# Where the down projections stand among the up projections of a feed-forward stage (fp32 split in two parts, four layers)

## The reference, cut to what matters

```python
# layers 0 and 1, D_FF = 2816
ffn = (jax.nn.silu(x @ w_ffn_gate[l]) * (x @ w_ffn_up[l])) @ w_ffn_down[l]
x = layer_norm(ALPHA * x + ffn, ln2_g[l], ln2_b[l])

# layers 2 and 3, D_FF_2 = 2816
u = h @ w_up                                   # both halves, 5632 columns
up = jnp.pad(u, ((0, 0), (CONV_WIDTH - 1, 0), (0, 0)))
c = conv_b
for j in range(CONV_WIDTH):
    c = c + conv_w[j] * up[:, j:j + S]
val, gate = jnp.split(c, 2, axis=-1)
x = x + (jax.nn.silu(gate) * val) @ w_down
```

## Time and profile before

| | us |
|---|---|
| median of 3 launches | 1415.01 |
| lowest, highest | 1412.89, 1415.77 |
| the profiled execution's own time | 1413.5 |
| span of its one core, first to last instruction | 1411.7 |

### The profile page before, as it was taken

The page is one execution under the profiler, slowest core; times in us unless marked ns, Lnnn a source line. Parts: engine busy times, 40 slices in busy tenths (PEclk is TensorE's granted clock), DMA queues, the critical chain, the costliest instruction groups (busy, mean ns, idle before and its releaser), DMA issues.

```text
span 1411.7 us, 24782 instructions
## 1 busy us (share of the span) xinstructions
PE 1362.0 (96%) x10120; PEld 1251.1 (89%) x10120; DVE 960.8 (68%) x1624; ACT 729.4 (52%) x1216; POOL 97.0 (7%) x79
## 2 busy tenths in 40 slices
PE   9998899999999988999998999999999999999998
PEld 8997699999899868999988998889998998889997
DVE  5766775555859577655575785688778555687776
ACT  5855443334486644433345555554556555654554
POOL 0330000000005100000000011011110000000000
PEclk9999999999999999999999999999999999999999
DMA  8851255555443314655544434535554533545451
GB/s 320 295 184 62 90 179 180 181 185 187 153 193 122 121 60 148 233 183 179 180 150 138 153 115 147 179 142 191 193 193 167 194 115 126 194 170 188 180 179 60
DMA packets 38632, 233.24 MB, mean 165 GB/s; under 512 B 5016, under 2 KB 8808, under 8 KB 12152
## 3 DMA queue, kind: packets, MB, share of 16 engines
q1 hardware_dynamic: 36456, 224.18, 45.5%
q0 software_dynamic: 2064, 7.47, 1.6%
HBM read 230.55 MB, written 1.09 MB: 164 GB/s over the span
## 4 chain that ended last, share of the span: by engine, by line
PE 82%; DVE 10%; ACT 5%; issue 2%; POOL 0%; DVEq 0%; ACTq 0%; POOLq 0%
PE bank L776 20%; PE bank L777 19%; PE bank L778 19%; PE bank L784 4%; PE bank L785 4%; PE bank L788 4%; DVE w_lo L603 3%; PE bank L910 1%; DVE arena L1770 1%; ACT w_hi L593 1%; PE bank L1000 1%; PE bank L1035 1%; PE bank L1022 1%; PE bank L885 1%; PE bank L927 1%
## 5 line engine op out<-in xcount | busy, mean ns | idle before, releaser
L603 DVE TENSOR_TENSOR w_lo<-raw,w_hi 128x1024 fp32r<-128x1024 f32 x404 | 489.3, 1249 | 99.0 <-ACT w_hi L593 94.0
L776 PE MATMUL bank<-a_hi,w_hi 128*128 128x256 f32 x1856 | 530.1, 286 | 5.2 <-DVE w_lo L603 5.2
L777 PE MATMUL bank<-a_lo,w_hi 128*128 128x256 f32 x1856 | 526.0, 283 | 0.0
L778 PE MATMUL bank<-a_hi,w_lo 128*128 128x256 f32 x1856 | 525.9, 283 | 0.0
L593 ACT ACTIVATE w_hi<-raw 128x1024 fp32r<-128x1024 f32 x404 | 406.1, 1050 | 90.1 <-PE bank L778 62.0
L776 PEld LDWEIGHTS bank<-a_hi,w_hi 128*128 128x128 f32 x1856 | 356.7, 192 | 10.7 <-issue 7.7
L777 PEld LDWEIGHTS bank<-a_lo,w_hi 128*128 128x128 f32 x1856 | 356.7, 192 | 1.2
L778 PEld LDWEIGHTS bank<-a_hi,w_lo 128*128 128x128 f32 x1856 | 356.7, 192 | 0.0
L1770 DVE SCALAR_TENSOR_TENSOR arena<-bank,conv_col,arena 128x254 f32<-128x254 f32 (+1 forms) x176 | 76.6, 476 | 46.4 <-ACT arena L1328 44.8
L784 PE MATMUL bank<-w_hi,a_hi 128*128 128x256 f32 (+1 forms) x320 | 99.4, 332 | 6.5 <-ACT a_hi L619 3.4
L777 PE MATMUL bank<-w_lo,h_hi 128*128 128x512 f32 x264 | 105.3, 399 | 0.0
(11 more groups left out here) (274 smaller groups left out, 1895.7 us busy)
## 6 DMA issues: line engine op xcount, KB each, us to landing
raw<-in_stream SPq DMA_DIRECT2D x201, 1024.0 KB, 4.9
bias_t<-bias_rows SPq DMA_DIRECT2D x6, 512.0 KB, 6.9
heads_buf<-in_w SPq DMA_DIRECT2D x2, 1024.0 KB, 8.7
gains<-in_w SPq DMA_DIRECT2D x2, 1024.0 KB, 10.7
gains<-in_ln_g POOLq DMA_DIRECT2D x4, 512.0 KB, 3.9
gains<-in_ln_b POOLq DMA_DIRECT2D x4, 512.0 KB, 5.6
gains<-in_rms_g POOLq DMA_DIRECT2D x3, 512.0 KB, 4.0
res<-in_xT SPq DMA_DIRECT2D x4, 256.0 KB, 4.8
```

The costliest lines, as they stand in the source:

```text
L603: dve.tensor_tensor(w_lo[:, i % PARTS, half_tile(h)], raw[:, i % SLOTS, half_tile(h)], w_hi[:, i % PARTS, half_tile(h)].bitcast(F32), ALU. ...
L776: pe.matmul(out, lh, rh, start=first, stop=False)
L777: pe.matmul(out, lh, rl, start=False, stop=False)
L778: return pe.matmul(out, ll, rh, start=False, stop=last)
```

## The change

`ffn_order` puts a down tile one pair of up tiles later. A constant LAG is 2, down tile r - 2 follows the up tiles 2r and 2r + 1, from r = 2 to r = 9. The new order is up0 up1 up2 up3 up4 up5 down0 up6 up7 down1 ... up18 up19 down7 up20 up21 down8 down9 down10. The tail stays three tiles, the inner slots six, the banks and the weight slots are as they were, and every engine follows the new order.

```diff
 HEAD = 2
 TAIL = 3
+LAG = 2
...
     for r in range(FT // 2):
         order += [("up", 2 * r), ("up", 2 * r + 1)]
-        if 1 <= r <= FT // 2 - TAIL:
-            order.append(("down", r - 1))
+        if LAG <= r < FT // 2 - TAIL + LAG:
+            order.append(("down", r - LAG))
     return order + [("down", FT // 2 - 3 + i) for i in range(TAIL)]
```

## The result

The changed kernel takes **1421.03 us** (median of five launches, 1420.36 to 1421.53) against 1415.01 us before; the ratio is 1.0040, with a 95% interval of 1.0028 to 1.0051. It is slower by 6 us, clear of noise, where 1420.3 was forecast. The profiled execution took 1421.03 us too, with a span of 1419.2 us, 7.5 us more than before; both numbers are of single executions.

The account below looks back on a forecast made before the run. TensorE, busy 96% of the span, was taken as the bound. 1.16 + 1.60 - 0.24 + 2.8 = +5.3 us on the profiled 1413.5 gave 1418.8, carried to the median 1420.3 us; range 1416.0 to 1424.0.

Parts of the forecast that it names:

- The bank of up4: Layers 2 and 3: up4 waits 3.83 us for up2's bank, replacing present waits; net +1.16 and +1.60 us.
- The waits that go: Layers 2 and 3: down0's wait for block 1's `h_hi` and the low-part waits vanish, 4.9 us removable at most.
- the 2.67 us: Layer 2, start of down0 to start of down2: time lost to waits before the change; layer 3 loses 2.23 us.
- The margins behind up4: Layers 2 and 3, tiles after up4: weight parts arrive with one to two us in hand, no further wait.
- the inner slots: Block 6 may be written once down0 ends, about 944; VectorE comes at about 953, so no wait and no cost.
- layers 0 and 1: Feed-forward stage there: up2's bank is free 2.9 and 1.3 us before up3 ends; no cost and no gain.
- the later rounds: Layers 2 and 3 after the start: rounds of two up tiles and one down tile stay at 17.10 us.
- The end of the stage: Layer 2 tail: down10 starts 0.47 us after the matmul before it; the extra goes, -0.24 us. Layer 3 has none.
- TensorE's clock: Behind the up4 wait in layers 2 and 3: clock drops to half, costing 1.4 us each, +2.8 us.
- The upper bound of 3.05 us a layer: Low-clock cost behind the up4 wait: at most half of 6.1 us, the longest low clock of four in the trace.
- The rival in which the clock stays up: Layers 2 and 3: bank wait with no low clock, 1417.5 us, or one, 1418.9; chance 0.22.
- The faster rival: Layers 2 and 3: up2's bank free in time, waits go and none comes, -4.9 - 0.24, 1409.9 us; chance 0.06.

Follow-up runs that it names:

- e4: Changed kernel plus 15 filling matmuls into free bank 4 ahead of up4 in layers 2 and 3; 1417.5 us, 1.0020 against the kernel before.
- e8: Changed kernel plus 8 filling matmuls into free bank 4 ahead of up4 in layers 2 and 3; 1418.2 us, 1.0025 against the kernel before.
- e9: The changed kernel run and profiled once more, unedited; 1420.5 us, 1.0040 against the kernel before.
- e3: Changed kernel with the banks of up4 and up5 exchanged in layers 2 and 3; 1417.6 us, 1.0020 against the kernel before.
- e1: Later down tiles in layers 0 and 1 only, old order in layers 2 and 3; 1415.2 us, 1.0005 against the kernel before.
- e2: Later down tiles in layers 2 and 3 only, old order in layers 0 and 1; 1421.8 us, 1.0051 against the kernel before.
- e5: Changed kernel; in layers 2 and 3 ScalarE and VectorE take block 2 first, splits threaded between blocks; 1409.6 us, 0.9966 against the kernel before.
- e10: Kernel before, old order, with block 2 ahead of blocks 0 and 1 for ScalarE and VectorE in layers 2 and 3; 1422.2 us, ratio 1.0057.
- e7: Changed kernel plus 4 filling matmuls into free bank 4 ahead of up4 in layers 2 and 3; 1419.0 us, 1.0026 against the kernel before.

## Why the prediction was right, and where it was off

**The bank of up4: right, to the place and the size.** The wait was put at the first matmul of up4, with the taps of up2 ending at 926.87 and up4 starting at 927.07, 3.83 us late; it was 926.86, 926.98 and 3.73 us (926.98 less 923.13 + 0.12). e4 and e8, where no low clock followed, show what is left without it: in layer 2 +0.96 and +0.94 us, in layer 3 +1.61 and +1.67. Take 0.43 of the slow time out of the two profiles of the changed kernel and they give the same within 0.1: +1.0 and +1.6 in the first, +1.0 and +1.6 in e9. Forecast were +1.16 - 0.24 = +0.92 and +1.60 us. e3 shows that it is the bank, as the exchange removes the wait, and e1 and e2 that it is these two layers.

**The waits that go: right.** `h_hi` of block 1 and the low parts of up4 and up5 no longer stop TensorE. Their 4.9 us were about all there was to have: e5, with no wait left, gets 5.01. One reading was incomplete: a third wait of layer 2, 0.23 us for a low part at 937.19, is in the 2.67 us but was not named.

**The margins behind up4, the inner slots, layers 0 and 1, the later rounds: right.** No further wait in the run of up tiles, rounds of 17.10 us, e1 equal to before within its interval. That layers 0 and 1 have no wait in this stage holds for the trace it was read from, but not for every execution: at up3 of layer 1 most of the other traces show a wait, up to 2.18 us, in either order.

**The end of the stage: right.** The tail of layer 2 was to lose its 0.24 us, and it did: in the changed kernel down10 starts 1083.66 - 1083.42 = 0.24 us behind the matmul before it, where it was 0.47.

```profile
1083.42 0.39 PE L779 MATMUL bank<-w_hi,h_lo 128*128 128x512 f32 x1
1083.66 0.50 PE L785 MATMUL bank<-w_hi,h_hi 128*128 128x512 f32 x1
```

**TensorE's clock: the right mechanism, mis-sized.** The term that missed is "1.4 us in each of layers 2 and 3, +2.8 us". It measured 2.60 and 2.33 us, 4.93 in all, in the profile of the changed kernel (e4 against it). Two errors stood against each other in it. The length of the low clock was taken from one row, 2.69 us, the shortest of four; behind the same idle it was 5.93, 5.29, 2.94, 3.10, 5.29 and 0 us in six instances, on average 3.8. And a slow us was counted as half lost, where 0.43 is. With the average the term would be 2 x 3.8 x 0.43 = 3.3 us and the sum +5.8, against the 6.0 of the medians. So the closeness of the forecast median, 1420.3 to 1421.03, is partly luck: between the two profiled executions the difference was 7.5 us and not 5.3, nearly all of the excess from this term, and the 1.5 us by which the profiled execution of before stood under its median happened to make up most of it. The upper bound of 3.05 us a layer held in all of them.

The rival in which the clock stays up was half seen: in e9 it did in one of two layers. The faster rival needed up2's bank ahead of 925.9, and e5 had it at 919.5, by another order of blocks: its figure, -4.9 us and less, came true there, but not through the change itself.

What stays open: why the launches of e3 lie 2 us above what its stretches say, what decides, execution by execution, whether and for how long the clock is down behind the wait, and which of e5's three parts its gain needs.

## What to carry to other kernels

Before work is moved later to give its input time, look at what takes its place: the down tile had been hiding the release of a bank, and the next tile wanted that bank at once. A lag and the order in which the engine behind frees its buffers belong together: each alone lost 5 to 7 us here, and both together, with the splits moved too, gained 5. Look also for the cheap part first: moving two splits in the old order gained 3 us. And price a new idle of the matmul engine of 2 us and more twice, once as the wait and once for the slow clock that may follow it.

## What the runs showed of the hardware beyond expectation

At 1.2 GHz the 256-column matmul started every 0.212 us and at 2.4 GHz every 0.120 us, so the slow clock cost 0.43 and not half of its time. Waits of 1.74 us (e8) and of 1.82 and 1.83 us (e3) ahead of an up tile left the clock up in both layers; 2.09 us (e2, layer 1), 2.36 us (e10) and 2.65 us (e7) brought it down each time; and 3.57 to 3.59 us did so in five of six instances, with 2.94 to 5.93 us of the work behind it slowed. The sixth, with the same idle, shows 1.00 throughout. The clock can fall within the wait, as in the changed kernel, or only behind the start of the next work, as 0.39 us behind it in layer 3 of e2.
